# Second attention of a two-layer encoder: the probabilities' low part behind each step's logits, the output transpositions behind the first dense group of the next pair

## The reference

```python
def sliding_window_gqa(h, w_qkv, sinks, rel_table, w_o):
    qkv = jnp.einsum('bsd,de->bse', h, w_qkv)
    ...
    s = jnp.einsum('bnqhgd,bnjhd->bhgnqj', q, kb).astype(jnp.float32)
    s = jnp.where(jnp.asarray(mask), s + bias, jnp.finfo(jnp.float32).min)
    m = jnp.maximum(jnp.max(s, axis=-1, keepdims=True), sink)
    p = jnp.exp(s - m)
    p = p / (jnp.sum(p, axis=-1, keepdims=True) + jnp.exp(sink - m))
    o = jnp.einsum('bhgnqj,bnjhd->bnqhgd', p.astype(v.dtype), vb).reshape(B, S, D)
    return jnp.einsum('bsd,de->bse', o, w_o)
```

## Time and profile before

| what | value |
|---|---|
| median of three runs | 1148.82 us (1148.69 to 1149.16) |
| the profiled execution, its own time | 1148.75 us |
| its span in the trace | 1147.1 us |
| TensorE busy | 1136.0 us, 99% |
| VectorE busy | 630.4 us, 55% |
| ScalarE busy | 504.8 us, 44% |
| GpSimd busy | 138.0 us, 12% |
| second attention, its eight steps | about 625 to 753 us from the span's start |

### The profile page before, as it was taken

One profiled execution on the slowest core, in us unless ns is written; L12 is line 12 of the kernel. 1 busy time (PEld: TensorE's weight loads), 2 busy tenths in 40 slices (PEclk: granted clock), 3 DMA queues, 4 the chain that ended last, 5 costly groups with the idle time before them and its releaser, 6 DMA issues.

```text
span 1147.1 us, 16682 instructions
## 1 busy us (share of the span) xinstructions
PE 1136.0 (99%) x5644; PEld 937.1 (82%) x5644; DVE 630.4 (55%) x1020; ACT 504.8 (44%) x908; POOL 138.0 (12%) x239
## 2 busy tenths in 40 slices
PE   9999999999999999999999999999999999999997
PEld 6888888888888888888887788888888888888886
DVE  7788887764442234444345778766444223444333
ACT  6777677553431223333334666645343122333221
POOL 6544341330000000000000322100000000000000
PEclk9999999999999999999999999999999999999998
DMA  6322331343223222322222212123322332232222
GB/s 225 97 89 92 91 91 55 96 120 105 91 92 102 100 91 92 107 94 90 93 91 92 51 53 59 52 74 95 107 91 92 100 102 92 91 107 95 91 92 92
DMA packets 34291, 106.98 MB, mean 93 GB/s; under 512 B 5760, under 2 KB 8096, under 8 KB 34256
## 3 DMA queue, kind: packets, MB, share of 16 engines
q1 hardware_dynamic: 29344, 98.61, 26.2%
q0 software_dynamic: 4768, 7.90, 2.9%
q10 hardware_dynamic: 144, 0.02, 0.0%
HBM read 103.84 MB, written 2.67 MB: 93 GB/s over the span
## 4 chain that ended last, share of the span: by engine, by line
PE 98%; DVE 1%; DMA 0%; ACT 0%; SPq 0%; issue 0%; DVEq 0%; ACTq 0%
PE acc L400 29%; PE acc L402 28%; PE acc L401 28%; PE s_ps L504 3%; PE om_ps L538 2%; PE pt_ps L708 2%; PE om_ps L562 1%; PE om_ps L534 1%; PE pt_ps L525 1%; PE om_ps L494 1%; PE s_ps L400 1%; PE s_ps L401 1%; PE s_ps L402 1%; DMA w_raw<-in_wstream 0%; PE om_ps L547 0%; DVE x_res L1304 0%
## 5 line engine op out<-in xcount | busy, mean ns | idle before, releaser
L802 ACT CAST w_hi<-w_raw 128x1024 fp32r<-128x1024 f32 x179 | 188.1, 1051 | 401.5 <-PE acc L402 395.1
L400 PE MATMUL acc<-h_hi,w_hi 128*128 128x512 f32 x792 | 318.4, 402 | 0.7 <-DVE w_lo L1086 0.7
L401 PE MATMUL acc<-h_lo,w_hi 128*128 128x512 f32 x792 | 308.9, 390 | 0.0
L402 PE MATMUL acc<-h_hi,w_lo 128*128 128x512 f32 x792 | 308.8, 390 | 0.0
L1086 DVE TENSOR_TENSOR w_lo<-w_raw,w_hi 128x1024 fp32r<-128x1024 f32 x177 | 217.9, 1231 | 143.7 <-ACT w_hi L802 143.0
L400 PE MATMUL acc<-u_hi,w_hi 128*128 128x512 f32 (+1 forms) x624 | 241.2, 387 | 0.0
L401 PE MATMUL acc<-u_lo,w_hi 128*128 128x512 f32 (+1 forms) x624 | 239.5, 384 | 0.0
L402 PE MATMUL acc<-u_hi,w_lo 128*128 128x512 f32 (+1 forms) x624 | 239.5, 384 | 0.0
L400 PEld LDWEIGHTS acc<-h_hi,w_hi 128*128 128x128 f32 x792 | 148.8, 188 | 37.5 <-issue 4.8
L402 PEld LDWEIGHTS acc<-h_hi,w_lo 128*128 128x128 f32 x792 | 148.7, 188 | 31.7
L401 PEld LDWEIGHTS acc<-h_lo,w_hi 128*128 128x128 f32 x792 | 149.1, 188 | 28.5 <-issue 0.7
(11 more groups left out here) (141 smaller groups left out, 1000.1 us busy)
## 6 DMA issues: line engine op xcount, KB each, us to landing
w_raw<-in_wstream SPq DMA_DIRECT2D x180, 512.0 KB, 3.3
bias_pairs<-rpb_reversed POOLq DMA_DIRECT2D x64, 62.0 KB, 2.4
bias_pairs<-t_shifted POOLq DMA_DIRECT2D x64, 48.0 KB, 2.2
x_res<-in_xT SPq DMA_DIRECT2D x8, 256.0 KB, 5.6
out_y<-x_res SPq DMA_DIRECT2D x8, 128.0 KB, 1.8
out_y<-x_res SPq DMA_DIRECT2D x4, 256.0 KB, 2.3
t_shifted<-vT POOLq DMA_DIRECT2D x16, 31.0 KB, 2.1
mask<-in_mask POOLq DMA_DIRECT2D x1, 64.0 KB, 5.5
```

Source lines behind the costliest of these rows:

```text
L400: nc.tensor.matmul(dst, a[0], b[0], start=start, stop=False)
L401: nc.tensor.matmul(dst, a[0], b[1], start=False, stop=False)
L402: return nc.tensor.matmul(dst, a[1], b[0], start=False, stop=stop)
L802: nc.scalar.copy(w_hi[:, c.odd, :], w_raw[:, c.odd, :]).then_inc(w_hi_made, 1)
```

## The change

On TensorE, the transposition of the first half of the outputs moves from phase 3 of its own pair to phase 0 of the next, and that of the second half from phase 1 to phase 2 of the next pair; both now stand behind the phase's first dense group and ahead of the scores. Behind the last step, the first half's stands between dense groups 13 and 14. On ScalarE the high parts of the outputs move to the end of phases 0 and 2. On VectorE the low part of the probabilities moves forward: only the logits of the phase, and in phases 1 and 3 the low part of the outputs, stay ahead of it. The two o_sums now follow it, the scaling of the queries comes in phase 1 in place of phase 2, and the queries' low part in phase 2 in place of phase 3.

```diff
--- before.py
+++ after.py
@@ -745,13 +745,13 @@
                     if before or n >= 1:
                         sw_transpose(*sw_unit_by(p, n, -1))
                     dense_part(2 * n)
+                    if n == 0 and before:
+                        transpose_o(p * 2 + (HEADS - 2), sw_bank(0))
+                    if n == 2 and before:
+                        transpose_o(p * 2 + (HEADS - 1), sw_bank(1))
                     if n < 3 or last != 8:
                         sw_scores(*sw_unit_by(p, n, 1))
                     dense_part(2 * n + 1)
-                    if n == 1 and before:
-                        transpose_o(p * 2 + (HEADS - 1), sw_bank(1))
-                    if n == 3:
-                        transpose_o(p * 2 + HEADS, sw_bank(0))
                     if before or n >= 1:
                         sw_values(*sw_unit_by(p, n, -1))
 
@@ -786,7 +786,9 @@
             sw_step(At(7), last=7)
             sw_step(At(8), last=8)
             sw_transpose(At(7), 3)
-            early_part(CH_SWO, GR_SWO, HEADS, 12, 16)
+            early_part(CH_SWO, GR_SWO, HEADS, 12, 14)
+            transpose_o(At(2 * HEADS - 2), sw_bank(0))
+            early_part(CH_SWO, GR_SWO, HEADS, 14, 16)
             sw_values(At(7), 3)
             output_projection(CH_SWO, GR_SWO, HEADS, 2 * BLOCKS, sw_bank(1))
             mlp(CH_MLP1, GR_MLP1, TI_MLP1, 3)
@@ -1018,17 +1020,17 @@
                 p = m + -1
                 for n in range(4):
                     sw_exp(p, n, 0)
-                    if n == 0 and before:
-                        sw_o_high(p + -1, 0)
-                    if n == 2 and before:
-                        sw_o_high(p + -1, 1)
                     if before or n >= 1:
                         sw_pt_high(*sw_unit_by(p, n, -1))
                     sw_exp(p, n, 1)
                     if n % 2 == 1:
                         sw_sinks(p, n // 2)
+                    if n == 0 and before:
+                        sw_o_high(p + -1, 0)
                     if n == 2 and dense:
                         tile_high(m + (GR_SW + 4), m + (TI_SW + 2), u_hi[:, 8 + m.odd, :])
+                    if n == 2 and before:
+                        sw_o_high(p + -1, 1)
                     if n == 3:
                         split_weights(m + (CH_SW + 6))
 
@@ -1071,8 +1073,8 @@
                 for n in range(2):
                     sw_step(At(2 + n, 2, i))
             sw_step(At(8), dense=False)
+            sw_pt_high(At(7), 3)
             sw_o_high(At(7), 0)
-            sw_pt_high(At(7), 3)
             split_weights(At(CH_SWO + 3))
             sw_o_high(At(7), 1)
             output_projection(CH_SWO, GR_SWO, 3)
@@ -1409,22 +1411,22 @@
                 p = m + -1
                 for n in range(4):
                     sw_logits(p, n)
-                    if n == 0 and before:
+                    if n == 1 and before:
                         sw_o_low(p + -1, 0)
-                    if n == 1 and before:
-                        sw_o_sum(p + -1, 1)
-                    if n == 2 and before:
+                    if n == 3 and before:
                         sw_o_low(p + -1, 1)
-                    if n == 2 and dense:
-                        scale_queries(m)
-                    if n == 3 and dense:
-                        queries_low(m)
-                    if n == 3:
-                        sw_o_sum(p, 0)
                     if before or n >= 1:
                         sw_pt_low(*sw_unit_by(p, n, -1))
                     if n == 0:
                         split_weights(m + (CH_SW + 5))
+                    if n == 1 and before:
+                        sw_o_sum(p + -1, 1)
+                    if n == 1 and dense:
+                        scale_queries(m)
+                    if n == 2 and dense:
+                        queries_low(m)
+                    if n == 3:
+                        sw_o_sum(p, 0)
                     if n == 3 and not dense:
                         split_weights(m + (CH_SW + 6))
 
@@ -1487,8 +1489,8 @@
                 for n in range(2):
                     sw_step(At(2 + n, 2, i))
             sw_step(At(8), dense=False)
+            sw_pt_low(At(7), 3)
             sw_o_low(At(7), 0)
-            sw_pt_low(At(7), 3)
             split_weights(At(CH_SWO + 3))
             sw_o_sum(At(7), 1)
             clear_squares(3)
```

## The result

The changed kernel takes 1154.37 us (median of 6 runs, 1154.10 to 1154.52), the kernel before 1148.78 (6 runs, 1148.66 to 1149.16): ratio 1.0048, 95% interval 1.0035 to 1.0061, 5.6 us more. The direction and the mechanism of the chain were as forecast; the size, +4.1, was too small, and the measured time lies 0.4 us above the top of the range.

A forecast was written before the change was run, and what follows sets the result against it. TensorE, busy 1136.0 of 1147.1 us, was taken as the bound. Stalls of 3.6 us in six steps, 0.3 in the first and 0.2 at the end gave +4.1 on 1148.75, so 1152.8 us; range 1150.3 to 1154.0.

The forecast's parts named there:

- the chain: Second attention: VectorE's new order delays unit 2's logits, then ScalarE's exponential and high part, making unit 1's values 0.63 us late.
- TensorE's waits were worth nothing to begin with: Values' weight loads, second attention: 8 of 9 waits (1.9 us in all) cost TensorE nothing; only the last leaves a hole.
- Rival 4: Values' weight loads, second attention: their 9 waits, 1.9 us, were TensorE's time and get freed; 1146.9 us, chance 0.03.
- The move on TensorE is free: Output transpositions on TensorE: a pair costs 0.21 us ahead of the scores as ahead of the values; bounds 0.10 and 0.33.
- the hole that I named: VectorE's idle time while it waits for the high part of unit 0; the moved output low part was to fit there.
- the term of 3.6 us: Six steps with queries still to scale and a pair before: a stall of 0.60 us each, 3.6 us in all.
- the 0.63 of the sum: Values of unit 1 on TensorE: forecast to start at 681.36, 0.63 us behind 680.73.
- It takes 1.47 (674.55 to 676.02): 670.18, where the next pair's logits start: VectorE, end of a step: the first half's o_sum takes 1.47 us and the next pair's logits follow at 670.18.
- a sign that its place is wrong: Check on the changed profile: holes at another unit, or at the scores, would prove the chain's place wrong.
- Case 1: The forecast itself: a stall of 0.4 to 0.75 us in each of six steps, 1151.6 to 1153.8 us; chance 0.68.
- Case 2: Smaller stall, 0.1 to 0.4 us a step, because full queues hand over faster: 1150.7 us; chance 0.15.
- Cases 3 and 5: 3: delay absorbed, only the end's 0.2 left, 1149.0, chance 0.10. 5: clock falls to its lower level, 1165, chance 0.04.

The follow-up runs named there:

- ScalarE's mend: Changed kernel, but in phase 2 ScalarE makes the high part of unit 1 ahead of the exponential of unit 2: 1150.16 us, ratio 1.0011.
- both mends: Changed kernel with scaling and queries' low part back in phases 2 and 3, and ScalarE's high part of unit 1 ahead of unit 2's exponential: 1149.15 us.
- the variant above: Changed kernel with VectorE's o_sums and scaling back in their old places, output transpositions and outputs' high and low parts left in their new ones: 1150.19 us.
- Taking 0.61 us out of it at the scaling: Changed kernel with VectorE's scaling of the queries back in phase 2 and their low part back in phase 3: 1150.36 us, ratio 1.0013.
- the loop written out: Changed kernel with VectorE's loop over the six middle steps unrolled, same instructions in the same order: 1152.66 us, ratio 1.0032.

## Why the prediction was right and where it was wrong

**TensorE's waits were worth nothing to begin with: right.** With ScalarE's mend alone, the loads at the values of unit 1 have no wait from the second step on, and the second value matmul still stands 0.29 us behind the dense one, as with the wait of 0.17 us before. With both mends the time is that of the kernel before (1.0002), although the loads of the values wait 2.6 us there. Rival 4 is out.

**The move on TensorE is free: right** (0.22 against 0.21 a pair, and six steps of 95.60 us with both mends against 95.63), with the reservation of the variant above: with VectorE's old order it costs some 0.15 us a step. In the change itself the low part of the outputs that moves with it fits the hole that I named, right behind the logits of unit 1.

**The chain: right in every link that was tried.** Taking 0.61 us out of it at the scaling brings back 4.0 us, cutting it at ScalarE 4.2 us. With the loop written out, the way from the transpositions of unit 2 to the load at the values of unit 1 takes 15.05 us (667.96 to 683.01); the prediction's terms add up to 15.14 (666.12 to 681.26). Its six steps take 98.70 us against 95.63 in the kernel before, 0.51 a step where I took 0.60; so the term of 3.6 us measures 3.1. The variant as a whole is 3.75 us over the kernel before, against the forecast of 4.1.

**Where luck helped.** The 0.62 us of TensorE at the values of unit 1 agree with the 0.63 of the sum only because 0.11 of them are the seam inside the loop's body, which the sum did not have; the chain by itself makes 0.49 to 0.54.

**The step of the prediction that failed** is "It takes 1.47 (674.55 to 676.02): 670.18, where the next pair's logits start". The o_sum's 1.47 us were read where a low part follows it inside a step. At the end of a step the next instruction comes 0.11 us later in the loop's body, 0.49 at its turn and 0.31 at its entry. Over seven seams that is 1.77 us which the sum put at nothing, and which the variant without the loop gives back (1.71). That, and not the chain, carries the time over the top of the range. In the trace of the kernel before, VectorE has no idle time that is put down to "issue", so no row could show it, and the low part of unit 2 stood at the seams. But I could have asked what that low part was hiding when the change takes it away, as I asked of every other cover.

**The rest of the sum.** From the span's start to the first scores of the stage the profiled execution was 0.27 us later than before (623.43 against 623.16 for the load of L504), in code that is the same; over all variants this moment lies between 623.07 and 623.62, so the 0.27 lie within the scatter. The first step cost 0.40 (0.3 forecast). From its values of unit 1 to those of the last step it is 116.29 us (633.47 to 749.76) against 111.58: 4.71, of which 3.6 were forecast. From there to the last output transpositions 15.36 against 15.12: 0.24 (0.2 forecast). The sum is 5.62, the spans differ by 5.6. The 4.71 are the chain, 3.1, and the seams as far as they reach TensorE, 1.7. The hole of the last step was misread as 0.28 us, where it is 0.54 from start to start; it stays in the changed kernel, so the sum does not suffer.

**Scores of unit 3.** I looked only at the values. The scores of unit 3 wait for the same logits, and in the steps behind a turn they are 0.35 us late (681.18 to 681.84 behind the transpositions, 0.31 without a wait). The prediction had named holes at the scores as a sign that its place is wrong. They are the seam's and not the chain's: with the loop written out the scores of unit 3 stand 0.55 us behind the dense matmul in every step, the plain distance with a pair between, while at the turns of the changed kernel it is 0.89 and 0.91. There they do not lengthen the step beyond the seam's 0.38, since the values of unit 1 wait for the chain anyway; with ScalarE's mend, where those values do not wait, they are the loss.

**Rivals.** Case 1 has the stall of each step right (0.4 to 0.75 us), and the time is over its end. Case 2 is not what came: handovers in the full queues were faster, but by 0.09 us over the whole chain, and the time went the other way. Cases 3 and 5 did not happen; the clock stayed at its upper level (2.4 GHz) through all the new holes, with 0.998 over the span and no slice of the page below 9 tenths. The swing between the levels, of which the Trainium skill, TensorE: Matmul & The Clock Gate, section "A second HAM failure mode: psum-queue depth-cycling", tells for another kernel, does not show in this trace, with one or two holes of 0.3 to 0.6 us in a step of 16.5 us.

## What to carry to other kernels

Where two engines hand tiles to each other in order, an instruction that is moved forward in one queue moves every other back, and the price shows on a third engine: follow the chain to the first instruction that the bottleneck waits for, and compare it with the time the bottleneck takes for the same stretch, since a chain that is just in time has no slack for 0.6 us. A wait in the profile of the bottleneck's loads is no loss until the spacing of its matmuls shows it. What stands last in a loop's body can matter: here an instruction of 0.87 us hid the loop's turn, and an o_sum of four short ones that wait for each other did not.

## What the runs showed of the hardware

Behind the o_sum, the turn of VectorE's loop costs 0.49 us, its entry 0.31, and a seam inside its body 0.11; with the loop written out all are 0, and behind the low part of 0.87 us they are 0 with the loop too. The Trainium skill, Advanced Engine Details and Errata, section "Control Flow Timing", gives some 51 ns for a plain branch and 108 ns for a compare and branch. The 0.49 us measured here are several times that, and no run here separates what they are made of.
